# First mixer, group norm: the four roots turned by VectorE and sent to all partitions through DRAM on GpSimd's queue

## The reference, cut to what matters

```
y = y.reshape(Bsz, S, D_INNER) * jax.nn.silu(z.astype(jnp.float32))
y = y.reshape(Bsz, S, SSM_GROUPS, D_INNER // SSM_GROUPS)      # 4 groups of 512
y = y * lax.rsqrt(jnp.mean(y * y, axis=-1, keepdims=True) + EPS)
y = y.reshape(Bsz, S, D_INNER) * g_out.astype(jnp.float32)
return y.astype(h.dtype) @ w_out
```

## Time and profile before

| what | value |
|---|---|
| profiled execution, its own time | 1801.43 us |
| span of the core in it | 1799.6 us |
| granted TensorE clock, mean | 0.999 of full speed |
| TensorE matmul busy | 1788.0 us, 99% |
| VectorE / ScalarE / GpSimd busy | 1057.3 / 737.2 / 72.7 us (59 / 41 / 4%) |

### The profile page before, as it was taken

How to read it: one execution, slowest core, us unless ns; L and a number is a source line. 1 busy time by engine, 2 the same in 40 slices (tenths; PEclk the granted TensorE clock), 3 DMA queues, 4 the chain that set the end, 5 groups by cost and what they waited for, 6 DMA issues and landing times.

```text
span 1799.6 us, 21075 instructions
## 1 busy us (share of the span) xinstructions
PE 1788.0 (99%) x8290; PEld 1448.1 (80%) x8290; DVE 1057.3 (59%) x1575; ACT 737.2 (41%) x1202; POOL 72.7 (4%) x127
## 2 busy tenths in 40 slices
PE   9999999999999999999999999999999999999998
PEld 7777777888766788888888888888888888888887
DVE  8899986577787576444333356664444654444333
ACT  5888885343477533232222432222222333222221
POOL 1002021000210000000000000000000000000000
PEclk9999999999999999999999999999999999999999
DMA  5476662333211233333333423333333233333331
GB/s 176 96 109 110 117 101 87 99 98 101 80 36 36 82 106 94 97 102 91 97 97 103 125 80 104 96 94 94 95 104 94 94 109 96 94 94 99 101 97 56
DMA packets 51425, 172.69 MB, mean 96 GB/s; under 512 B 6208, under 2 KB 8768, under 8 KB 51328
## 3 DMA queue, kind: packets, MB, share of 16 engines
q1 hardware_dynamic: 47376, 161.44, 29.3%
q0 software_dynamic: 3088, 9.20, 5.2%
q10 hardware_dynamic: 864, 0.72, 0.1%
HBM read 169.15 MB, written 2.18 MB: 95 GB/s over the span
## 4 chain that ended last, share of the span: by engine, by line
PE 94%; DVE 4%; ACT 1%; issue 1%; DMA 0%; SPq 0%; DVEq 0%; ACTq 0%
PE pb L761 28%; PE pb L763 28%; PE pb L762 28%; PE pb L872 2%; PE pb L973 2%; PE pb L1002 1%; PE pb L978 1%; PE pb L1130 1%; PE pb L1129 1%; PE pb L1131 1%; DVE CV L1759 0%; DVE wl L1541 0%; PE pb L1139 0%; DMA raw<-in_ssm_in 0%; PE pb L824 0%
## 5 line engine op out<-in xcount | busy, mean ns | idle before, releaser
L761 PE MATMUL pb<-XR,wr 128*128 128x512 f32 x1584 | 624.2, 394 | 0.1
L762 PE MATMUL pb<-XL,wr 128*128 128x512 f32 x1584 | 616.9, 389 | 0.0
L763 PE MATMUL pb<-XR,wl 128*128 128x512 f32 x1584 | 616.8, 389 | 0.0
L1541 DVE TENSOR_TENSOR wl<-raw,wr 128x1024 fp32r<-128x1024 f32 (+1 forms) x297 | 358.0, 1205 | 342.1 <-ACT wr L1187 341.1
L1187 ACT ACTIVATE wr<-raw 128x1024 fp32r<-128x1024 f32 (+1 forms) x295 | 305.6, 1036 | 316.8 <-PE pb L763 291.7
L761 PEld LDWEIGHTS pb<-XR,wr 128*128 128x128 f32 x1584 | 297.4, 188 | 65.2 <-issue 3.9
L763 PEld LDWEIGHTS pb<-XR,wl 128*128 128x128 f32 x1584 | 297.3, 188 | 62.5
L762 PEld LDWEIGHTS pb<-XL,wr 128*128 128x128 f32 x1584 | 297.5, 188 | 60.7 <-issue 0.2
L761 PE MATMUL pb<-ffn2HR,wr 128*128 128x512 f32 (+1 forms) x198 | 72.7, 367 | 0.0
L762 PE MATMUL pb<-ffn2HL,wr 128*128 128x512 f32 (+1 forms) x198 | 72.3, 365 | 0.0
L763 PE MATMUL pb<-ffn2HR,wl 128*128 128x512 f32 (+1 forms) x198 | 72.3, 365 | 0.0
(11 more groups left out here) (370 smaller groups left out, 2266.3 us busy)
## 6 DMA issues: line engine op xcount, KB each, us to landing
raw<-in_ffn_in SPq DMA_DIRECT2D x88, 512.0 KB, 3.5
raw<-in_mix_in SPq DMA_DIRECT2D x48, 512.0 KB, 3.5
raw<-in_ssm_in SPq DMA_DIRECT2D x40, 512.0 KB, 4.1
raw<-in_ffn_out SPq DMA_DIRECT2D x32, 512.0 KB, 3.6
DB<-cum POOLq DMA_DIRECT2D x28, 256.0 KB, 8.7
raw<-in_ffn_out SPq DMA_DIRECT2D x16, 384.0 KB, 3.1
raw<-in_mla_in SPq DMA_DIRECT2D x11, 512.0 KB, 3.3
raw<-in_ssm_out_a SPq DMA_DIRECT2D x8, 512.0 KB, 3.3
```

Source lines behind the costliest of these rows:

```text
L761: e.matmul(o, r, xr, start=first, stop=False)
L762: e.matmul(o, r, xl, start=False, stop=False)
L763: return e.matmul(o, l, xr, start=False, stop=last)
L1541: e.tensor_tensor(wl[j % NS][:, 0:width(j)], raw[j % NR][:, 0:width(j)], wr[j % NS][:, 0:width(j)].bitcast(F32), ALU.subtract).then_inc(s_ ...
```

## The change

The spreading by TensorE is dropped. Each group's roots are written into the first four columns of `QB` (128x32, zero elsewhere). One tile after its `gsum` VectorE turns `QB` block by block (32x32) into `QT32` (`gturn`), so that partitions 32q to 32q+3 hold the 512 roots in rows of 32. GpSimd's queue writes them to a DRAM tensor `grows` with four DMAs, waits for these, and reads them back to all 128 partitions into `CH` (a tile of the decay stage, free by then) with one DMA of 256 KB. `gscale` reads `CH` instead of a PSUM bank. In the tail, `gscale` of group 2 moves from step 1 to step 3, `gturn` of group 3 is put at step 3, and `gscale` of group 3 moves from step 5 to step 7.

```diff
@@ ssm_steps()
             if x[1][0] == "gsum":
+                due.append((no + 1, ("gturn", x[1][1])))
                 due.append((no + (5 if x[1][1] == 0 else 3), ("gscale", x[1][1])))
...
-    tail = {0: [("gfold", 3)], 1: [x[1] for x in due] + [("gsum", 3)], 5: [("gscale", 3)]}
+    tail = {0: [("gfold", 3)], 1: [("gsum", 3)], 3: [x[1] for x in due] + [("gturn", 3)], 7: [("gscale", 3)]}
@@ TensorE
-            elif what == "gscale":
-                spread(f"g{m[0]}")
@@ VectorE
             elif what == "gscale":
-                key = f"spread g{m[0]}"
-                w.wait_ge(*bk.full[key])
+                w.wait_ge(s_grow, 16 * m[0] + 16)
                 for t in range(4 * m[0], 4 * m[0] + 4):
                     e.scalar_tensor_tensor(out=YN[:, t, :], in0=YN[:, t, :], scalar=col("g_out", t),
-                                           in1=PB[bk.bank[key]][:, :], op0=ALU.mult, op1=ALU.mult).then_inc(s_ynorm, 1)
+                                           in1=CH[:, :].bitcast(F32), op0=ALU.mult, op1=ALU.mult).then_inc(s_ynorm, 1)
+            elif what == "gturn":
+                w.wait_ge(s_groot, m[0] + 1)
+                e.transpose(QT32[m[0] % 2][:, :], QB[:, :]).then_inc(s_gturn, 1)
@@ GpSimd
-        for key, dst in (("g0", GN), ("g1", GN), ("g2", GN), ("g3", GN)):
+        for key, dst in (("g0", QB), ("g1", QB), ("g2", QB), ("g3", QB)):
             for h in ahead.get(key, ()):
                 spread_decay(h)
             w.wait_ge(s_sv, taken[key])
-            if key in ("g1", "g2", "g3"):
-                w.wait_ge(s_spread, spreads[key])
+            root4 = dst[:, 0:4]
+            g = int(key[1])
+            if g == 0:
+                w.wait_ge(s_zero, 2)
+            else:
+                w.wait_ge(s_gturn, g)
...
+            w.wait_ge(s_gturn, g + 1)
+            for q in range(4):
+                e.dma_start(grows[g][:, q, :], QT32[g % 2][32 * q:32 * q + 4, :]).then_inc(s_gout, 16)
+            w.wait_ge(s_gout, 64 * g + 64)
+            if g == 0:
+                w.wait_ge(s_dec, 4)
+            else:
+                w.wait_ge(s_ynorm, 4 * g)
+            e.dma_start(CH[:, :].bitcast(F32),
+                        grows[g:g + 1].rearrange("a i q j -> a (i q j)").to_broadcast([128, S])).then_inc(s_grow, 16)
```

More of the change, by code:

```diff
@@ L453, in columns_of @@
         return rows[row_no[key]].rearrange("(c q) j -> (q j) c", q=4)
+    grows = nc.dram_tensor("grows", (4, 4, 4, 32), F32, kind="Internal").ap()
     def col(name, i=0):
@@ L474, in build_in @@
     s_groot, s_root, s_spread, s_rs, s_vroot = [sem("s_" + n) for n in ("groot", "root", "spread", "rs", "vroot")]
+    s_gout, s_grow, s_gturn, s_zero = [sem("s_" + n) for n in ("gout", "grow", "gturn", "zero")]
     s_const, s_warm = sem("s_const"), sem("s_warm")
@@ L521, in build_in @@
     conv_no = {n: i for i, n in enumerate(convs)}
-    spreads = {n: i for i, n in enumerate(("x", "g0", "g1", "g2", "g3", "fin0", "fin1"))}
+    spreads = {n: i for i, n in enumerate(("x", "fin0", "fin1"))}
     sums_no = {n: i + 1 for i, n in enumerate(("x", "g0", "g1", "g2", "g3", "fin0", "fin1"))}
@@ L525, in build_in @@
     rooted.update({n: (s_groot, i + 1) for i, n in enumerate(("g0", "g1", "g2", "g3"))})
-    root_of = {n: GN for n in ("g0", "g1", "g2", "g3")}
     taken = {n: i + 1 for i, n in enumerate(("x", "g0", "g1", "g2", "g3", "fin0", "fin1"))}
@@ L586, in build_in @@
                     bk.place("sum " + s, 3, (s_sums, sums_no[s]), (s_sv, taken[s]))
-                elif side == "gscale":
-                    s = f"g{m[0]}"
-                    bk.place("spread " + s, tring.next(), (s_spread, spreads[s] + 1), (s_ynorm, 4 * m[0] + 4))
         elif what == "y":
@@ L593, in build_in @@
         bk.place(("oa", n), 4 + n, whole("ssm_out_a", 7), (s_res, n + 1))
-    bk.place("spread g2", 2, (s_spread, spreads["g2"] + 1), (s_ynorm, 12))
     bk.place("sum g3", 3, (s_sums, sums_no["g3"]), (s_sv, taken["g3"]))
-    bk.place("spread g3", 2, (s_spread, spreads["g3"] + 1), (s_ynorm, 16))
     ring = Ring([0, 1, 2, 4])
@@ L782, in spread @@
             w.wait_ge(*rooted[key])
-            r4 = root_of.get(key, RN)
             for i in range(4):
-                m = e.transpose(o[:, 128 * i:128 * i + 128], r4[:, i:i + 1].to_broadcast([128, 128]), ident[:, :])
+                m = e.transpose(o[:, 128 * i:128 * i + 128], RN[:, i:i + 1].to_broadcast([128, 128]), ident[:, :])
             m.then_inc(s_spread, 1)
@@ L2194, in _ @@
         for q in (QA, QB):
-            e.memset(q[:, :], 0.0).then_inc(c.up(), 1)
+            e.memset(q[:, :], 0.0).then_inc(s_zero, 1)
         for i in range(2):
@@ L2329, in _ @@
             w.wait_ge(s_sv, taken[key])
-            if key in ("g1", "g2", "g3"):
-                w.wait_ge(s_spread, spreads[key])
-            e.tensor_scalar(dst[:, :].bitcast(I32), GV[:, :].bitcast(I32), -0.5, float(0x5F3759DF), ALU.mult,
+            root4 = dst[:, 0:4]
[4 more added lines that the diff above has]
+                w.wait_ge(s_gturn, g)
+            e.tensor_scalar(root4.bitcast(I32), GV[:, :].bitcast(I32), -0.5, float(0x5F3759DF), ALU.mult,
                             ALU.add).then_inc(c.up(), 1)
@@ L2335, in _ @@
                 w.wait_ge(c.h, c.n)
-                e.tensor_tensor(GW[:, :], dst[:, :], dst[:, :], ALU.mult).then_inc(c.up(), 1)
+                e.tensor_tensor(GW[:, :], root4, root4, ALU.mult).then_inc(c.up(), 1)
                 mul(GW, GW, GV)
@@ L2340, in _ @@
                 w.wait_ge(c.h, c.n)
-                e.tensor_tensor(dst[:, :], dst[:, :], GW[:, :], ALU.mult).then_inc(s_groot if i == 2 else c.up(), 1)
+                e.tensor_tensor(root4, root4, GW[:, :], ALU.mult).then_inc(s_groot if i == 2 else c.up(), 1)
+            w.wait_ge(s_gturn, g + 1)
[8 more added lines that the diff above has]
+                        grows[g:g + 1].rearrange("a i q j -> a (i q j)").to_broadcast([128, S])).then_inc(s_grow, 16)
         def row_out(key):
```

## The result

The changed kernel takes 1809.05 us (median of 5 runs, 1806.89 to 1810.12), the kernel before 1801.41 (1801.33 to 1801.95): ratio 1.0039, 95% interval 1.0028 to 1.0050. It is slower by 7.6 us where 3.3 were forecast, where the forecast had given 0.44 to slower and 0.52 to a change within 0.2%. The median lies 0.45 us above the upper end of the range (1808.6); as a ratio, 1.0039 against the 1.0040 of that end, it lies just inside. The profiled execution took 1809.05 us itself, for a span of 1807.3.

The account below looks back on a forecast made before the run. TensorE, with matmuls busy 99% of the span, was taken to bound the kernel. Terms +2.5 (group 0), +1.7 (group 1) and -0.9 (groups 2 and 3) made +3.3 on 1801.43, so 1804.7 us; range 1799.6 to 1808.6.

Parts of the forecast that it names:

- Four spreads, -1.76 us: TensorE's chain: each dropped spread saves 0.44 us, four together 1.76 us.
- Banks "can only free earlier": TensorE's PSUM banks: turns and mixes no longer share two banks with spreads, so these can only free earlier; no size.
- Group 0, VectorE's wait: At group 0's turning, VectorE waits for GpSimd's root, taking 3.6 us, and goes on 6.9 us late (bounds 6.8 to 10.6).
- rival B: Group 0: GpSimd's root stays at 7.5 us though VectorE waits; 1808.4 us, chance 0.13.
- What is late next: After group 0: TensorE waits 1.4 us at step 6; ScalarE's silu 4.8 late; tile 26's turn 2.5 late, spread included.
- Group 1, the fetch for h = 28: Behind group 1's broadcast: fetch issued 3.9 us late, landing 2.9 slower; ScalarE 3.9 late, TensorE's group 2 sum 1.7 late.
- Sum: Whole kernel: adds the groups' terms, +2.5, +1.7 and -0.9, to +3.3 us, giving 1804.7 us.
- Groups 2 and 3: Tail: broadcasts cost TensorE nothing, at most 0.6 us; two dropped spreads give back 0.88 us.
- a sign of being wrong: Tail: the forecast called itself wrong if VectorE waits for `CH` there; no size set.
- Rival E: Tail: group 3's broadcast lands in 11.6 us, stopping TensorE 4.7 us more; 1809.4 us, chance 0.06.
- Rivals C and D: C: fetch h = 28 has room, only group 0 costs, 1802.6 us, 0.15. D: all new waits hidden, 1799.7, 0.12.
- A: The forecast itself: stalls at both group 0 and group 1; 1804.7 us, own range 1803.0 to 1806.5, chance 0.50.

Follow-up runs that it names:

- experiment 3: Changed kernel with rows 28 and 29 fetched before the wait for group 1's writes, and group 0 turned three tiles behind its sum: 1800.24 us, ratio 0.9994.
- experiment 4: Kernel before, spreads kept and no broadcast, with VectorE waiting one tile after group 0's sum for GpSimd's root: 1806.92 us, ratio 1.0030.
- experiment 1: Changed kernel with the fetches of decay rows 28 and 29 issued between group 1's four writes and the wait for them: 1802.43 us, ratio 1.0006.
- Experiments 6 to 8: Kernel of experiment 3 with 2, 4 or 8 needless VectorE instructions ahead of group 2's last fold: 1803.39, 1805.94 and 1809.28 us.

## Why the prediction was off, point by point

- **Four spreads, -1.76 us:** right. The ledger has -0.48 for one, and experiment 3 has 1.1 of the 1.76 left over with a wait of 0.33.
- **Banks "can only free earlier":** right, and worth more than thought: with the spreads kept, the same lateness of VectorE brings a wait of 2.73 us at a spread, and half clock behind it (experiment 4).
- **Group 0, VectorE's wait:** right. 6.46 us measured for 6.6 to 6.9, ended by the root; the root took 3.57 us for 3.6. So rival B is out. The rule of the two SBUF inputs from the Trainium skill ("SBUF — State Buffer", Who interferes with whom) agrees with the trace: with VectorE parked, every one of the 13 instructions takes about 0.2 us, where beside a busy VectorE single ones took up to 1.14.
- **What is late next:** right in place and order. TensorE came 1.24 us late to step 6 (1.4 predicted) and 1.83 to the turning of tile 26 (2.5 predicted), the start's 0.65 taken off. ScalarE's silu there started at 193.07, 4.0 us late for a predicted 4.8. Experiment 3 against 1 gives 2.2 for the waits without the spread; the prediction's 2.5 with the spread would make 2.9.
- **Group 1, the fetch for h = 28:** the late fetch and its way to TensorE were right; the terms in between were wrong and nearly cancelled, which was luck. The issue was late by 5.6 us (251.37, with before's 243.26 shifted by 2.5) for 3.9: writes of 0.5 KB take 2.6 us to land in the median and 3.4 at most, where the rows had 1.6. Row 28 then landed in 8.2 us and did not pay the 2.9 put down for following the broadcast; row 29, for which the prediction had no term, took 13.2. ScalarE ended 4.5 us late for 3.9. TensorE was set back 2.97 us at the sum, 2.5 with the spread counted in, for 1.7 (bounds 0 and 3.1). The 2.6 us for 256 KB, the estimate by the Trainium skill ("DMA: Bandwidth & Descriptors", Anatomy of one DMA), is low even for the broadcast alone (3.6 at the least), as the prediction said.
- **The step that failed** is "Sum": it prices TensorE's waits at their length and has no term for the clock. The wait of 2.82 us was followed by some 7 us at half clock, 3.34 us in the ledger. With it the sum would have read about 1808. What else was off makes 1.0 us: 0.65 at the start of the program, -0.7 at group 0, +0.8 at group 1, and 0.3 of the last two spreads. That the kernel is TensorE's again after the first mixer held. Experiments 6 to 8 show that the wait alone does it, experiment 1 that taking the wait away gives all of it back. The trace of before could have warned twice: none of its waits inside the mixer is over 1 us, so its clock of 0.999 says nothing about longer ones; and in its last stretch, where TensorE waits 1.05 and 1.37 us and has little else to do, the clock does fall (busy time by stretches, kernel before):

```profile
1790.00:1795.00 5.00, 2.02 (x15) 1.52 (x13) 2.40 (x9) 0.59 (x2) 0.00 (x0) 0.97 0.28 91
1795.00:1799.00 4.00, 0.00 (x0) 0.00 (x0) 1.70 (x5) 0.00 (x0) 1.41 (x2) 0.50 0.80 262
```

- **Groups 2 and 3:** right in what TensorE pays, which is nothing: VectorE's YL came in time, and TensorE's timeline has no wait of over 0.1 us from 300 to 350 us, in the changed kernel or in experiment 3. But VectorE waited 1.07 us for `CH` at group 3, which the prediction had named as a sign of being wrong. The sign was set too sharply. Rival E is out.
- **Rivals C and D** are out in the changed kernel; D's number nearly comes back in experiment 3, once both waits are taken away.
- **Range and chances:** the prediction's own bounds add up to +1.1 to +9.0, which holds the measured +7.6, but the range was drawn only up to B. The numbers of B (1808.4) and E (1809.4) lie nearer to the result than A's, and neither mechanism took place. The chances within 0.2% add up to 0.55 and not 0.53.

What stays open: why the half clock costs 1.6 us in one execution and some 3.1 in another; no run separates the wait's length from where it falls in time. Nor is it shown what between 0.95 and 2.43 us of wait is the least that brings it.

## What to carry to other kernels

A wait on a TensorE that is never idle is not priced by its length. In these profiles waits up to 1 us cost just themselves; from 2.4 us on the half clock behind them cost 1.6 to 3.3 us more. So list a change's new waits and ask which of them would be the longest that TensorE has had.

A queue that works in order has two prices for a round trip through DRAM: what stands behind its waits (here two fetches, 4 us late for 6.6 us of run time), and what shares it in flight. Put the due fetches between the issue of the writes and the wait for them; a fetch ahead of the writes made them land in 8.4 us. And place a consumer's wait behind the root, not beside it: two tiles later it cost TensorE nothing. Later is not better everywhere: the scaling a tile later gained nothing, because that spot lay on the chain between ScalarE and VectorE.

## What the runs showed of the hardware that was not expected

- Stalls of TensorE of 2.4 to 4.4 us were followed by half clock (0.50) for 3.4 or 6.8 us, which begins 0.2 to 2 us after TensorE is busy again and costs 1.6 or some 3.2 us; with 6.3 us the clock fell during the stall. The busy share does not show it: a scan step took 4.0 to 4.5 us instead of 2.37.
- Of a burst of 256 KB reads on GpSimd's queue, the first decay row lands 7.8 to 8.5 us behind its issue, as without the burst. What is issued within 3 us behind it takes 10.7 to 13.3, a decay row (8.7 in the kernel before) or a broadcast (3.6 when issued ahead of the rows).
- Four writes of 0.5 KB to DRAM: 0.52 us each to issue, 1.6 to 3.4 us to land in the changed kernel, and 8.4 when they are issued 1 us behind a decay row (experiment 3).
